# Decode attention of a hybrid decoder layer: lane maxima per token with one reduction per step, and the first norm in three ranges of tokens

## What is computed

```python
h = rms_norm(x, norm_mix)
proj = h @ w_in
fq, fk, fv, ff, gq, gk, gv, ga, gb, gz = jnp.split(proj, SPLIT_POINTS, axis=-1)
lf = jax.nn.log_sigmoid(ff + b_forget)
k_all = jnp.concatenate([past_k, fk], axis=1)
v_all = jnp.concatenate([past_v, fv], axis=1)
cum = jnp.cumsum(jnp.concatenate([past_lf, lf], axis=1), axis=1)
fox_out = fox_attention(fq, k_all, v_all, cum[:, p_len:], cum, pos[p_len:], pos)

def one_block(args):
    s = jnp.einsum('bqhd,bkhd->bhqk', q_blk, k) * scale
    s = s + (cq_blk[..., :, None] - ck_t[:, :, None, :])
    s = jnp.where(mask, s, NEG_BIG)
    p = jax.nn.softmax(s, axis=-1)
    return jnp.einsum('bhqk,bkhd->bqhd', p, v)
```

## Time and profile before

| | us |
|---|---|
| runs: median (lowest, highest) | 1908.2 (1907.02, 1912.01) |
| profiled execution | 1911.62 |
| its span | 1910.0 |
| setup | 0 to 66.78 |
| gates | 66.78 to 128.04 |
| fox, steps 0, 1, 2, 3 begin at | 128.04, 269.20, 418.78, 569.53 |
| fox, last `weigh_values` ends | 709.65 |
| fox ends | 744.80 |
| gdn ends, dense begins | 1029.5 |
| mean granted TensorE clock over the span | 0.923 |

### The profile page before, as it was taken

How to read it: one execution, slowest core, us unless ns; L and a number is a source line. 1 busy time by engine, 2 the same in 40 slices (tenths; PEclk the granted TensorE clock), 3 DMA queues, 4 the chain that set the end, 5 groups by cost and what they waited for, 6 DMA issues and landing times. The chain is left out here.

```text
span 1910.0 us, 30732 instructions
## 1 busy us (share of the span) xinstructions
PE 1664.6 (87%) x10909; PEld 1571.7 (82%) x10909; DVE 933.8 (49%) x1794; ACT 684.5 (36%) x1089; POOL 541.0 (28%) x340
## 2 busy tenths in 40 slices
PE   4498797898799653898994999999999999999997
PEld 4487686787688532896993999999999999999997
DVE  6425537646646554537324545444444444544444
ACT  3323543553453441224234333222222222445344
POOL 4411222232223111623300222222222222544541
PEclk6699999899899865998996999999999999999999
DMA  3324244244243224400005431111111111211122
GB/s 102 117 75 133 70 136 137 80 135 134 67 145 115 69 96 160 175 1 25 23 1 216 133 100 44 44 44 47 52 44 44 44 49 50 106 51 45 45 67 89
DMA packets 211045, 158.16 MB, mean 83 GB/s; under 512 B 23201, under 2 KB 199233, under 8 KB 209872
## 3 DMA queue, kind: packets, MB, share of 16 engines
q1 hardware_dynamic: 168492, 120.48, 20.3%
q10 hardware_dynamic: 41656, 31.92, 5.5%
q0 software_dynamic: 784, 4.31, 0.6%
HBM read 123.95 MB, written 32.89 MB: 82 GB/s over the span
## 5 line engine op out<-in xcount | busy, mean ns | idle before, releaser
L176 PE MATMUL ps<-x_hi,w_hi 128*128 128x344 f32 x1584 | 508.3, 321 | 1.1 <-issue 1.1
L177 PE MATMUL ps<-x_lo,w_hi 128*128 128x344 f32 x1584 | 505.7, 319 | 0.0
L178 PE MATMUL ps<-x_hi,w_lo 128*128 128x344 f32 x1584 | 505.6, 319 | 0.0
L176 PEld LDWEIGHTS ps<-x_hi,w_hi 128*128 128x128 f32 x1584 | 297.6, 188 | 3.0 <-issue 1.4
L178 PEld LDWEIGHTS ps<-x_hi,w_lo 128*128 128x128 f32 x1584 | 298.0, 188 | 0.0
L177 PEld LDWEIGHTS ps<-x_lo,w_hi 128*128 128x128 f32 x1584 | 297.3, 188 | 0.1
L176 PE MATMUL ps<-h_hi,wm_hi 128*128 128x344 f32 x672 | 226.8, 337 | 0.2
L177 PE MATMUL ps<-h_lo,wm_hi 128*128 128x344 f32 x672 | 218.7, 325 | 0.0
L178 PE MATMUL ps<-h_hi,wm_lo 128*128 128x344 f32 x672 | 218.4, 325 | 0.0
L2284 POOL TENSOR_TENSOR w_lo<-w_raw,w_hi 128x1024 fp32r<-128x1024 f32 x42 | 110.1, 2621 | 371.2 <-ACT w_hi L2452 371.2
L2288 POOL TENSOR_TENSOR w_lo<-w_raw,w_hi 128x512 fp32r<-128x512 f32 x44 | 112.1, 2554 | 134.7 <-ACT w_hi L2495 134.7
(11 more groups left out here) (366 smaller groups left out, 2908.7 us busy)
## 6 DMA issues: line engine op xcount, KB each, us to landing
w_raw<-in_w_up SPq DMA_DIRECT2D x44, 512.0 KB, 3.9
k_past<-in_cache_k SPq DMA_DIRECT2D x256, 64.0 KB, 1.9
v_past<-in_cache_v SPq DMA_DIRECT2D x256, 64.0 KB, 2.0
wm_raw<-in_w_in ACTq DMA_DIRECT2D x28, 512.0 KB, 4.1
w_raw<-in_w_down SPq DMA_DIRECT2D x44, 256.0 KB, 2.7
gdn_scratch<-conv ACTq DMA_DIRECT2D x12, 528.0 KB, 3.1
g_qkv<-gdn_scratch SPq DMA_DIRECT2D x12, 528.0 KB, 9.9
x_scratch<-xT POOLq DMA_DIRECT2D x1, 4128.0 KB, 11.4
```

The costliest lines, as they stand in the source:

```text
L176: pe.matmul(out, w_hi, a_hi, start=first, stop=False)
L177: pe.matmul(out, w_hi, a_lo, start=False, stop=False)
L178: return pe.matmul(out, w_lo, a_hi, start=False, stop=last)
```

## The change

Three parts, in one edit.

1. **Lane maxima.** `dec_score` subtracts each lane's own maximum at once, so the exp can follow in the same slot and needs no reduction. The reduction over lanes is made once per step for all 8 tokens (`all_max(j)`, in slot 0 of the next step); from it come, per step, one factor per lane and token (`factor_logs`, `exp_factors`), which weighs the lane's sum (`lane_weights`) and, as the moving operand of the product with V's page sums, its values. `past_values` runs once per step (1 product with ones, 8 with the page sums kept in `v_sum`). `weigh` and `sum_pages` come one slot earlier. V has two buffers; `load_v` waits for the page sum of token n−2.
2. **First norm by ranges of tokens** (384, 384 and 264 columns). TensorE sums the squares of each block straight from `sq`, VectorE's reduction goes; factor, scaling and both parts are made per range; VectorE makes all low parts, ScalarE stores x by range.
3. **Gates.** Their weights are loaded and split in setup (the raw ones lie in a tile `front`, which later holds `q_wide` and the diagonal tiles); in the gates stage TensorE begins without waiting for a split, and six pieces instead of three go before the past bias. Pages of `cache_logf`: 27 on SP in setup and 21 in gates, 16 on POOL.

The core of the diff:

```diff
-EARLY_PAGES, POOL_PAGES = 28, 20
+EARLY_PAGES, POOL_PAGES = 27, 16
...
+            def sum_squares(n):
+                if n == 0:
+                    pe.wait_ge(ones_ready, 1)
+                if n == 2 * RANGE:
+                    pe.wait_ge(logs_out, 1)
+                pe.wait_ge(blk_squared, n + 1)
+                out = sums(n)
+                for k in range(KC):
+                    mm = pe.matmul(out, v.ones[:], sq[:, n % 2, k, 0:out.shape[-1]], start=(k == 0), stop=(k == KC - 1))
+                mm.then_inc(blk_summed, 1)
...
+            copy_out(0)
+            dve.wait_ge(wg_split, 1)
+            for a, n, c in GATE_COLS:
+                dve.tensor_tensor(wg_lo[:, :, c:c + n], wg_raw[:, :, a:a + n], wg_hi[:, :, c:c + n].bitcast(F32), ALU.subtract)
+            dve.wait_ge(norms_turned, 1)
+            dve.tensor_copy(v.norms[:].rearrange("p k n -> p (k n)"), ps[:, 4, 0:3 * KC])
+            for n in range(1, 5):
+                copy_out(n)
+            normalise(0)
+            for n in range(5, 8):
+                copy_out(n)
+            normalise(1)
+            copy_out(8)
...
+            normalise(2)
...
-            for g in range(NG):
-                tiles.project(pe, 0, g)
+            for q in range(6):
+                tiles.project(pe, q // NG, q % NG)
             pe.wait_ge(past_loaded[0], 16 * (NPG - POOL_PAGES))
...
             def load_v(n, pages):
-                need(sp, dval_done, 0, n - 2)
+                need(sp, v_summed, 0, n - 1)
...
-            def past_values(n):
-
-                need(pe, v_summed, 0, n + 1)
-                need(pe, dval_out, 0, n)
-                if n % DEC == DEC // 2:
-                    need(pe, normed, n // DEC, 1)
-                pe.matmul(ps[:, 7, 0:16], v.ones[:], score[:, n % DEC].rearrange("p g h -> p (g h)"), start=True, stop=True)
-                pe.matmul(ps[:, 7, 16:17], v_past[:, n % 3, 0], v.ones[:, 0:1], start=True, stop=True).then_inc(dval_done.sem, 1)
+            def past_values(j):
+
+                need(pe, den_ready, j, 1)
+                need(pe, v_summed, j, DEC)
+                need(pe, normed, j, 1)
+                pe.matmul(ps[:, 7, 0:2 * DEC], v.ones[:], lane_sum.rearrange("p b h -> p (b h)"), start=True, stop=True)
+                for b in range(DEC):
+                    mm = pe.matmul(ps[:, 7, 2 * DEC + 2 * b:2 * DEC + 2 * b + 2], v_sum[:, b], lane_factor[:, b], start=True, stop=True)
+                mm.then_inc(dval_done.sem, 1)
...
-            def all_max(n):
-                b = n % DEC
-                need(pool, dmax_ready, 0, n + 1)
+            def all_max(j):
+                need(pool, dsub_ready, j, DEC)
                 settle(pool, "pool")
-                pool.partition_all_reduce(d_all[:, b], d_max[:, b], P, RMAX).then_inc(dmax_all.sem, 1)
+                pool.partition_all_reduce(d_all.rearrange("p b h -> p (b h)"), lane_max[:, j % 2].rearrange("p b h -> p (b h)"), P, RMAX).then_inc(dmax_all.sem, 1)
...
-                    if 0 <= n - 1 < PAST:
-                        all_max(n - 1)
+                    if j and i == 0:
+                        all_max(j - 1)
...
-                    if 0 <= n - 2 < PAST:
-                        weigh(n - 2)
+                    if 0 <= n - 1 < PAST:
+                        weigh(n - 1)
...
-                dve.tensor_reduce(d_max[:, b], score[:, b].rearrange("p g h -> p h g"), AX.X, ALU.max).then_inc(dmax_ready.sem, 1)
...
+                top = lane_max[:, j % 2, b]
+                dve.tensor_reduce(top, score[:, b].rearrange("p g h -> p h g"), AX.X, ALU.max)
                 dve.drain()
-                dve.tensor_tensor(score[:, b], score[:, b], d_max[:, b].unsqueeze(1).broadcast_to([P, PAGES, 2]), ALU.subtract)
-                dve.tensor_tensor(d_self[:, j % 2, b], d_self[:, j % 2, b], d_max[:, b], ALU.subtract).then_inc(dsub_ready.sem, 1)
+                dve.tensor_tensor(score[:, b], score[:, b], top.unsqueeze(1).broadcast_to([P, PAGES, 2]), ALU.subtract).then_inc(dsub_ready.sem, 1)
...
                 need(dve, v_weighed, 0, n + 1)
...
+                need(dve, dval_done, n // DEC, 0)
...
+            def factor_logs(j):
+                need(dve, dmax_all, j, 1)
+                dve.tensor_tensor(d_all, d_all, d_self[:, j % 2], ALU.max)
+                dve.drain()
+                dve.tensor_tensor(lane_factor, lane_max[:, j % 2], d_all, ALU.subtract)
+                dve.tensor_tensor(self_factor, d_self[:, j % 2], d_all, ALU.subtract).then_inc(fsub_ready.sem, 1)
```

More of the change, by code:

```diff
@@ L162, in program @@
             v.allocate_act("h1", act_scope)
-            setup(nc, t, v, past_loaded)
+            with ExitStack() as scope:
+                gate_w = [sb(n, [P, KC, GROWS], F32R, scope) for n in ("wg_hi", "wg_lo")]
+            front = sb("front", [P, SEQ + 4 * P + KC * 16], F32, act_scope)
+            gate_w.append(front[:, SEQ + 4 * P:].rearrange("p (k n) -> p k n", k=KC))
+            setup(nc, t, v, past_loaded, gate_w)
             with ExitStack() as scope:
                 tiles = Tiles(t, v, scope)
-                gates(nc, t, v, past_loaded, tiles)
-                fox(nc, t, v, tiles)
+                gates(nc, t, v, past_loaded, tiles, gate_w)
+                fox(nc, t, v, tiles, front)
         free_semaphores()
@@ new lines, in scale, with lower, normalise @@
+            def scale(r, cols, k):
+                dve.scalar_tensor_tensor(out=tmp[:, k, cols], in0=xT[:, k, cols], scalar=v.norms[:, k, 0:1],
+                                         in1=rstd[:, cols], op0=ALU.mult, op1=ALU.mult).then_inc(normed, 1)
+            def lower(r, cols, k):
+                dve.wait_ge(high, KC * r + k + 1)
+                dve.tensor_tensor(v.lo[:, k, cols], tmp[:, k, cols], v.hi[:, k, cols].bitcast(F32), ALU.subtract).then_inc(low, 1)
+            def normalise(r):
+                cols = RANGES[r][1]
+                dve.wait_ge(rstd_ready, r + 1)
+                for k in range(KC + 2):
+                    if k < KC:
+                        scale(r, cols, k)
+                    if k >= 2:
+                        lower(r, cols, k - 2)
@@ L416, in norm_pool @@
-def norm_pool(pool, v, S, tmp, ranges):
-    for r, cols in ranges:
-        for k in range(1, KC, 2):
-            pool.wait_ge(S["hi"], r * KC + k + 1)
-            ins = pool.tensor_tensor(v.lo[:, k, cols], tmp[:, k, cols], v.hi[:, k, cols].bitcast(F32), ALU.subtract)
-        ins.then_inc(S["odd_lo"], 1)
-def gates(nc, t, v, past_loaded, tiles):
+                width = P if n < NBLK else DEC
+                act.activation(sq[:, n % 2, :, 0:width], xT[:, :, tokens(n)], ACT.Square).then_inc(blk_squared, 1)
@@ new lines, in upper, with save @@
+            def upper(r):
+                cols = RANGES[r][1]
+                for k in range(KC):
+                    act.wait_ge(normed, KC * r + k + 1)
+                    act.activation(v.hi[:, k, cols], tmp[:, k, cols], ACT.Copy).then_inc(high, 1)
+            def save(r):
+                cols = RANGES[r][1]
+                act.dma_start(v.x_dram[:, :, cols], xT[:, :, cols]).then_inc(x_saved, 16)
+            for n in range(XS):
+                load_x(n)
+            act.wait_ge(wg_loaded, 32)
@@ new lines, in _ @@
+            act.wait_ge(wg_zeroed, 1)
+            for a, n, c in GATE_COLS:
+                ins = act.activation(wg_hi[:, :, c:c + n], wg_raw[:, :, a:a + n], ACT.Copy)
+            ins.then_inc(wg_split, 1)
+            for n in range(NBLK + 1):
+                square(n)
+                load_x(n + XS)
+                if n == 3:
+                    factor(0)
+                    save(0)
+                if n == 4:
+                    upper(0)
+                if n == 6:
+                    factor(1)
+                    save(1)
+                if n == 7:
+                    upper(1)
@@ L430, in gates @@
+            factor(2)
+            save(2)
+            upper(2)
+            act.wait_ge(x_saved, 48)
+def gates(nc, t, v, past_loaded, tiles, gate_w):
     with ExitStack() as scope:
@@ L526, in _ @@
         def _(pe):
-            pe.wait_ge(split_lo, 1)
             for g in range(NG):
@@ L781, with fox @@
 PAST = STEPS * DEC
-VALUES_AFTER = 4
-def fox(nc, t, v, tiles):
+def fox(nc, t, v, tiles, front):
     with ExitStack() as scope:
```

273 lines of the change are left out of this document (112 added, 161 removed).

## The result

| | before | after | ratio (95% interval) |
|---|---|---|---|
| median of runs, us | 1908.28 (1907.02 to 1912.01) | 1876.73 (1874.61 to 1879.51) | 0.9838 (0.9823 to 0.9853) |
| profiled execution, us | 1911.62 | 1876.69 | |
| span, mean granted clock | 1910.0, 0.923 | 1875.1, 0.940 | |

What follows compares the result with a forecast made beforehand. POOL's reductions stall VectorE and so TensorE, a chain and not a load. Setup −1.8, gates −5.3, steps 0 to 2 −48, step 3 −20, tail −9 make −84.1: 1827.5 profiled, 1824 us against the median; range 1788 to 1866.

Steps and rivals of the forecast that it cites:

- The bound before: Attention: a chain through POOL's 32 reductions over partitions, not load, holds TensorE, idle 19.7 us in a middle step.
- Steps 0 to 2: Attention: one reduction per step instead of eight; −14 us in step 0, −17 in each of steps 1 and 2, −48 together.
- 7 left: TensorE's idle time remaining in a middle attention step, from 19.7 us; −12.7 us.
- The lower clock: Attention: slow matmuls behind a stall, 11 us at about half pace, become rarer; −3.5 us per middle step.
- Step 3: Last attention step: half of TensorE's 39.2 us idle time goes; −20 us (bounds −10 and −33).
- Tail: Behind the attention steps: one token left to weigh and sum, one reduction with nothing behind it on POOL; −9 us.
- New waits in the attention: Past values wait in slot 2 for lane weights and page sums; costed at nothing, otherwise one 6 us stall per step.
- Gates: Gates stage: TensorE begins at the stage's start instead of 5.8 us after it; −5.3 us (−3 to −5.8).
- Setup: Setup: norm by three token ranges, last factor by 57, end at 65; −1.8 us (bounds −9 and +6).
- The taps take over: Rival, attention: VectorE's row in slots with convolution taps, slowed by POOL or not, sets the slot; −50 us, 1858; chance 0.20.
- V's two buffers: Rival, attention: V's loads, waiting for the page sum two tokens before, set the pace; 1960 us, slower; chance 0.04.
- one of the signs named for being wrong: Attention: V loads named as what weighing waits for would show the forecast wrong.

Runs made afterwards that it cites:

- Run 9: Kernel before, reductions in place, with one of the three multiply-adds of each tap group on VectorE: 1916.99 us against 1910.38, 1.003.
- run 1: Kernel before, each of the 32 reductions over partitions replaced by an ordinary POOL multiplication by ones: 1879.47 us against 1911.99, 0.9837.
- Run 3: Changed kernel with one of the three multiply-adds of each convolution tap group on VectorE: 1828.33 us, 0.9574 of the kernel before.
- runs 11: Changed kernel with POOL's weighing held back in slots 1, 2 and 4 until VectorE has finished the slot's taps: 1853.44 us, 0.9715.
- run 12: Changed kernel with early lane weights, and POOL's split of weights and weighing held back in slots 1, 2 and 4 until the taps are done: 1845.27 us, 0.9648.
- Run 5: Changed kernel with lane weights made before the taps of slot 1 instead of behind the score rounding of slot 2: 1875.48 us, 0.9813.
- run 8: Changed kernel with early lane weights, taps of slots 2 and 4 behind the next slot's first score round, V's load ahead of K's on SP: 1873.67 us, 0.9798.
- run 10: Kernel before with the change's setup and gates, each reduction an ordinary POOL multiplication by ones, three V buffers: 1876.78 us, 0.9834.

## Why the prediction was wrong

**The bound before: right.** Run 9 shows that the reduction held TensorE and the taps did not; run 1 that its stalls could be taken away.

**Steps 0 to 2, the step that failed:** "TensorE keeps what does not come from the reduction: the wait of the score rounding behind the taps, 3.63 before and taken at 1.5 to 2 per tapped slot, since the taps no longer start 6 us late", and with it "I take 7 left of 19.7". What was said to go did go: TensorE's wait in front of `weigh_values` in these steps fell from 19.0 to 1.4 us. What it keeps was mis-sized: all its other idle time, 38.7 us before, was taken to fall to some 21 and rose to 43.2. It took a cover away and priced what lay under it as smaller than it had been seen. The waits of the score rounding before were 4.3, 3.9, 3.6, 3.0, 3.6 and 3.2 us, two per step, and the 7 left hold room for one of 1.5 to 2 per step (with 3.4 for the squares and 1 to 2 of small ones); measured were 5.8 and 3.1 in step 0, then 3.1 and 0.2, and 2.2 and 3.1, and the lane weights took 2.8 and 1.6 more. In step 0 there was little to win: only 2.3 of its 16.9 us of idle time stood before `weigh_values`, and of the 14 forecast 3.0 came.

The whole term was −48 and measured −14.4. Idle time fell by 13.1 us of the 37 or so that the term holds, the busy time of TensorE by 1.3 instead of 10.5. The lower clock was not paid less often: in step 1 its mean is 0.93 in both kernels. Before, it was 0.52 in two stretches, the 11 us of the earlier trace rows and 7 us behind a wait of 3.04; in the changed kernel it is 0.50 in the 7.3 us behind the wait of 2.83 and 0.72, 0.69 and 0.68 in the 5 us or so behind waits of 3.54, 3.06 and 2.14.

Why the row did not shorten: durations of VectorE's operations were read from rows in which POOL was standing still, 311 us of waiting, and were then used for a kernel in which it works beside them. Run 3 reaches the forecast: its four steps are 65.6 us shorter than before, where 68 were forecast. Against the changed kernel they are 43 us shorter; runs 11 and 12 recover 27 and 32 of these by keeping POOL out of the way, with every tap in place. What is left between run 12 and run 3 was not taken apart.

**Step 3:** −20 forecast, −8.2 measured, the same term: run 3 has −20.8 there.

**Tail:** −9 forecast, −9.9 measured, in part by luck. The prediction has nothing behind the last reduction on POOL, but the weighing of the last token stands there and waits 7.07 us for the way back. **New waits in the attention:** costed at nothing; the past values wait 2.83, 1.64 and 1.28 us in steps 1 to 3. Run 5 takes these waits away and gains nothing clear of noise, but its taps are stretched more (1835 ns in the mean), so it does not price them alone.

**Gates:** as forecast. The stage's first matmul is at 67.69 instead of 72.58, 0.3 us behind the last low part, and from there to the attention it is 55.3 us, as before (55.5). **Setup:** −1.8 forecast, so an end at 65; the last low parts end at 67.4. In the changed kernel:

```profile
26.08 1.28 ACT L417 ACT_TABLE_LOAD   x1
...
27.37 0.52 ACT L417 ACTIVATE rstd<-rstd 128x384 f32<-128x384 f32 x1
...
58.37 0.42 ACT L417 ACTIVATE rstd<-rstd 128x264 f32<-128x264 f32 x1
...
60.36 0.51 DVE L392 COPY gconv<-ps 128x336 f32<-128x336 f32 x1 [7.70 <-PE ps L347]
...
61.30 1.29 DVE L362 SCALAR_TENSOR_TENSOR h_tmp<-xT,norms,rstd 128x264 f32<-128x264 f32 x3
```

The factor of the last range is there at 58.8, but VectorE has the copies of the parameters in front, which wait 7.70 us for their turning on TensorE, and starts at 61.30. The chain left these copies out: 2.5 us. The factor itself came 1.8 us later than the 57 of the forecast. The table load takes 1.28 us, begins 0.07 us behind the end of the Ln (26.01), and the Exp begins with the load's end. The drain of about 1380 ns per switch that the Trainium skill (ScalarE: Activation LUTs, What ACT_TABLE_LOAD costs) adds to the load is not seen in these rows.

**The rivals.** "The taps take over" was the right mechanism, given 0.20 and −50; the stages it named gave −14.4, −8.2, −9.9 and −5.0. It left out the price that made it win, the stretching by POOL, although its own sentence names it. V's two buffers did not decide: POOL waits 100.9 us for V, one of the signs named for being wrong, but run 8 halves that wait and is no faster, and run 10, with three buffers, has the time of the changed kernel.

## What to carry to other kernels

A stall that is taken away uncovers the next one: before a wait's whole idle time is counted as gain, shorten in a run what stands right behind it, and see whether that alone gives anything (here nothing with the stall and 48 us without). Durations read while a neighbouring engine stands still are not those of a kernel in which it works; where VectorE and POOL both read SBUF, an engine that hardly appears among the waits can set the pace. Here a wait that keeps POOL away from the critical row (the taps) was worth 23 to 31 us, and the other order of that row, with POOL still beside it, 6.

## What the runs showed of the hardware

VectorE and POOL stretch each other, whole operations at a time. In the changed kernel's row above, the first tap takes 1.31 us from 300.63 and the weighing that comes 0.13 us behind it lasts longer by about what was left of that tap; the second tap, at 302.03, takes 2.79 and ends 1.1 us after the weighing does (303.71); the diagonal then lasts 1.75 instead of 0.75. The Trainium skill (SBUF — State Buffer, Who interferes with whom) says that a VectorE instruction with two inputs in SBUF contends with a GpSimd instruction that reads SBUF, and that the ports which the two share are an exclusive lock. These rows agree with it: each operation lasts longer by about what was left of the other when it began. They agree also in what is not stretched: the `TENSOR_REDUCE` with its one input (5 of its 32 in the changed kernel have POOL beside them and take 1.22 us like the others) and the score roundings with an input in PSUM (351 ns mean in both kernels, 350 in the 6 that have POOL beside them). How small the victim is does not matter: the 128x16 operation, 175 ns where POOL does nothing, took up to 2.3 us beside it, and its mean in step 1 went from 204 to 599.
